# The order of high and low matmuls in the experts' third to eighth group: pairs once a unit, once a half or twice a half, the other k-tiles in turn

## The chip, the cores and the metric

The kernel runs on one core of a Trainium2 chip. The metric is the device time of one execution in microseconds, the median of several runs. The names of the engines are those of the profile: PE (TensorE matmul), PEld (its weight load), DVE (VectorE), ACT (ScalarE), POOL (GpSimd), SP (SyncE, which issues the weight DMAs).

## What is computed

A sequence of 256 tokens with 2048 features passes two blocks in fp32. The first block is a norm, a projection, a pooling mixer beside a gated recurrence, a projection back, and then a layer of 16384 single-neuron experts. The second block has attention, a depthwise convolution, gates and a feed-forward of 8192 features. The part that the change touches is the layer of experts:

```python
u = jnp.take(peer_u, expert, axis=0)
act = jax.nn.gelu(jnp.einsum('chkd,cd->chk', u, zc))
v = jnp.take(peer_v, expert, axis=0)
w = (gate * act.astype(jnp.float32)).astype(zc.dtype)
return jnp.einsum('chk,chkd->cd', w, v).astype(zc.dtype)
```

The kernel computes it densely: all 16384 experts in eight groups of 2048, with a gate that is zero where a token has not chosen the expert.

## The kernel before

All large products are cut into 544 **units**, numbered in the order in which they run. A unit makes 128 output features for 256 tokens. It has two **halves** (p = 0, 1) of 8 **k-tiles** of 128 x 128 weights, so 16 k-tiles. `STAGE` tells for each unit the stage, its number i in the stage, and the group c. In the layer of experts each group c (0 to 7) has 16 units "u" (first product, operand `ZA`) and 16 units "v" (second product, operand `ZB`). The third to eighth group (c = 2 to 7) are the units 120 to 311, and u and v stages follow one another, 16 units each. Later stages in that form are the feed-forward's "up" and "dn" (units 416 to 543).

To keep fp32 precision with fp32r operands, a weight tile is split: `hi` is the rounded weight, `lo` is the rest. The operand is split in the same way and stands as 512 columns, 256 rounded and 256 of rest. A k-tile is therefore two matmuls into one PSUM bank `G`: `high` (L413, `hi` by all 512 columns) and `rest` (L417, `lo` by the first 256 columns). They take 128 x 128 weights each, so each has a weight load of its own.

**Weights.** SP loads one half (512 KB) into a ring of 8 `raw` buffers, and waits for `s_mm`, by which PE tells that a half is done. ACT rounds it into a ring of 7 `hi` buffers (L676). DVE subtracts into `lo`, which lies over `raw` (L1054). `walk` fixes where ACT and DVE prepare halves (two a unit, about two and a half units ahead of PE) between the parts of the evacuation.

**Results.** There are four banks. ACT copies the columns 256 to 511 out (L683) and DVE adds them to the first 256 (L1060). For a unit u of group 2 on, POOL scales, ACT takes gelu, POOL multiplies by the gate, ACT rounds to `ZB` and DVE makes the rest (L1125). A v unit then adds to `X`. The first v unit of a group waits for its operand k-tile by k-tile (`operand_ready`, semaphore `s_zu`).

**The order on PE.** `half` (L437) issues the 8 k-tiles of a half in steps. In a step of 1 it issues high, low. In a step of 2 it issues high, high, low, low, which is called a **pair** here; several k-tiles one by one are **in turn**. PE waits for the high weights ahead of the first high matmul (`s_hi`), and for the low weights ahead of the first low one (`weights_ready`, `s_lo`). `at_once` (L426) gives the step. Before the change it is 2 in the u units of groups c >= 2 and in all v units but the first of a group (i = 0), where it is 1. In the "up" and "dn" stages it is 1. Three places with several units at once go through `group` and take all in turn.

Of the kernel before, what the change touches and what calls it, by code (L numbers as in the profile page):

```python
# [36 lines left out]
F0, SG, MG, YO = 312, 352, 384, 400  # L37
# [127 lines left out]
def build(nc, ins, out):  # L165
    ctx = ExitStack()
    with ctx:
# [80 lines left out]
        qkv, VT, mask, neg = zb["qkv"], zb["VT"], zb["mask"], zb["neg"]  # L248
# [60 lines left out]
        def weights(u, p):  # L309

            st, i, c = STAGE[u]
            ks = range(8 * p, 8 * p + 8)
            if st == "lx":
                return ins["w_in"][8 + i, p], ZA, ks
            if st == "pl":
                return ins["w_in"][2 * POOL_G[i // 2] + i % 2, p], ZA, ks
            if st == "gt":
                return ins["w_in"][16 + i, p], ZA, ks
            if st == "ot":
                return ins["w_out"][i, p], ZB, ks if p else OUT_ORDER  # L320
            if st == "wq":
                return ins["wq"][i, p], ZA, ks
            if st == "u":
                return ins["pu"][16 * c + i, p], ZA, ks
            if st == "v":
                return ins["pv"][i, 2 * c + p], ZB, ks
            if st == "gb":
                return ins["w_in2"][32 + i, p], ZA, ks
            if st == "ga":
                return ins["w_in2"][24 + i, p], ZA, ks  # L330
            if st == "qkv":
                return ins["w_in2"][8 * c + i, p], ZA, ks
            if st == "sg":
                return ins["w_in2"][40 + 16 * c + i, p], ZA, ks
            if st == "mg":
                return ins["w_sc"][i, p], ZB, ks
            if st == "yo":
                return ins["w_o"][i, p], ZA, ks
            if st == "up":
                return ins["w_up"][16 * c + i, p], ZA, ks  # L340
            return ins["w_down"][i, 2 * c + p], ZB, ks
# [28 lines left out]
        def tensor_program(pe):  # L370
            def operand_ready(u, k):
                st, i, c = STAGE[u]
                if u == LX:
                    pe.wait_ge(s_zx, k + 1)
                elif u == OT and k < 8:
                    pe.wait_ge(s_zp, OUT_ORDER.index(k) + 1)
                elif u == OT:
                    pe.wait_ge(s_zg, k - 7)
                elif u == WQ:
                    pe.wait_ge(s_zh, k + 1)  # L380
                elif u in VB[:2] and k % 2 == 0:
                    pe.wait_ge(s_za, 8 * c + k // 2 + 1)
                elif u in VB[2:]:
                    pe.wait_ge(s_zu, 16 * (c - 2) + k + 1)
                elif u == F0:
                    pe.wait_ge(s_zi, k + 1)
                elif u == MG and k < 8:
                    pe.wait_ge(s_zo, k + 1)
                elif u == MG:
                    pe.wait_ge(s_zc, k - 7)  # L390
                elif u == YO:
                    pe.wait_ge(s_zm, k + 1)
                elif u == M0:
                    pe.wait_ge(s_zr, MIX_OF[k] + 1)
                elif u in DNB:
                    pe.wait_ge(s_zf, 16 * c + k + 1)

            def weights_ready(h):
                pe.wait_ge(s_lo, h + 1)

            def bank_free(b):
                if b >= 4:
                    pe.wait_ge(s_join, b - 3)

            def high(u, p, k, G, first):

                w = hi[POS[u][p] % NW][:, k % 8, :]
                Z = weights(u, p)[1]
                if u == N - 1:
                    pe.matmul(G[:, 0:256], w, Z[:, k, 0:256], start=first, stop=False, skip_group_check=True)  # L410
                    pe.matmul(G[:, 0:256], w, Z[:, k, 256:512], start=False, stop=False, skip_group_check=True)
                else:
                    pe.matmul(G[:, 0:512], w, Z[:, k, :], start=first, stop=False, skip_group_check=True)  # L413

            def rest(u, p, n, k, G, last):

                m = pe.matmul(G[:, 0:256], lo[POS[u][p] % NRAW][:, k % 8, :], weights(u, p)[1][:, k, 0:256], start=False,  # L417
                              stop=last, skip_group_check=True)
                if n == 7:
                    m.then_inc(s_mm, 1)  # L420
# [2 lines left out]
                high(u, p, k, G, first)  # L423
                rest(u, p, n, k, G, last)

            def at_once(u):  # L426

                st, i, c = STAGE[u]
                if st in ("ot", "v", "mg", "yo"):
                    return 2 if i else 1  # L430
                if st == "u":
                    return 2 if c >= 2 else 1
                if st in ("gb", "ga", "qkv", "sg"):
                    return 2 if u > F0 else 1
                return 1

            def half(u, p):  # L437
                apart = STAGE[u][0] == "mg"
                b = BANK[u] + (p if apart else 0)
                start, stop = apart or p == 0, apart or p == 1  # L440
                if start:
                    bank_free(b)
                ks = list(enumerate(weights(u, p)[2]))
                step = at_once(u)
                for x in range(0, 8, step):
                    for n, k in ks[x:x + step]:
                        operand_ready(u, k)
                        if n == 0:
                            pe.wait_ge(s_hi, POS[u][p] + 1)
                        high(u, p, k, GB[b % 4], n == 0 and start)  # L450
                    if x == 0:
                        weights_ready(POS[u][p])
                    for n, k in ks[x:x + step]:
                        rest(u, p, n, k, GB[b % 4], n == 7 and stop)

            def group(u):
                units = range(u, u + GROUPS[u])
                for w in units:
                    bank_free(BANK[w])
                for p in range(2):  # L460
                    for n, k in enumerate(range(8 * p, 8 * p + 8)):
                        operand_ready(u, k)
                        for w in units:
                            if n == 0:
                                weights_ready(POS[w][p])
                            product(w, p, n, k, GB[BANK[w] % 4], p == 0 and n == 0, p == 1 and n == 7)
# [113 lines left out]
            for u in range(N + 1):  # L580
# [5 lines left out]
                if u in GROUPS:  # L586
                    group(u)
                elif u not in INSIDE:
                    half(u, 0)
                    if 68 <= u < 84:  # L590
                        spread(2 * (u - 68))
                    half(u, 1)
# [1151 lines left out]
        @block.tensor  # L1744
        def _(e):
            tensor_program(e)
# [73 lines left out]
```

## Time and profile before

| | |
|---|---|
| median of 3 runs | 3238.07 us (3237.05 to 3240.23) |
| the profiled execution | 3243.61 us, span 3241.8 us |
| PE busy | 3161.9 us, 98% of the span |
| PEld busy | 2762.4 us, 85% |
| DVE, ACT, POOL busy | 2180.3, 1693.5, 676.1 us |
| granted TensorE clock, mean | 0.99 |
| HBM | 189 GB/s over the span |
| high matmuls (L413) | 52% of the chain that ended last |
| low matmuls (L417) | 26% of that chain |

Matmuls overlap: a high one is shown as 0.40 us long though the next may start 0.23 us after it. So the starts are read here, not the lengths. In the timeline two matmuls of one kind in a row are merged into one line (x2), which makes pairs easy to see: a line with x2 highs, a line with x2 lows.

### The profile page before, as it was taken

How to read it: one execution, taken by the hardware profiler on the slowest of the kernel's cores; microseconds unless marked ns; L12 is line 12 of the kernel's file. 1: busy time of each engine (PE TensorE's matmuls, PEld its weight loads, DVE VectorE, ACT ScalarE, POOL GpSimd, SP SyncE). 2: the span in 40 equal slices, each digit the busy share in tenths (PEclk: the TensorE clock that was granted, in tenths of full speed). 3: DMA queues.
4: the chain of work that ended last, by engine and by line, in shares of the span. 5: the costliest groups of instructions: out<-in, count | busy, mean ns of one | idle time of the engine just before them, and what ended most of it. 6: DMA issues, size and time to landing. Idle time of an engine off the chain costs nothing.

```text
span 3241.8 us, 46963 instructions
## 1 busy us (share of the span) xinstructions
PE 3161.9 (98%) x18222; PEld 2762.4 (85%) x18222; DVE 2180.3 (67%) x3000; ACT 1693.5 (52%) x2629; POOL 676.1 (21%) x690
## 2 busy tenths in 40 slices
PE   8999989999999999999999999999998999999998
PEld 7788878888888888888888888888887888888887
DVE  7857999864655555565646569999675855555564
ACT  6554457544544445454545655566656544444444
POOL 1423320321312222131313410000242100000003
PEclk9999989999999999999999999999999999999999
DMA  6555547656666666566666665555665566666664
GB/s 241 156 189 177 181 150 234 232 184 211 189 215 189 215 189 215 188 215 189 189 215 189 189 187 162 174 163 184 189 191 163 170 190 191 191 188 190 190 191 138
DMA packets 177853, 615.35 MB, mean 190 GB/s; under 512 B 18272, under 2 KB 35040, under 8 KB 176224
## 3 DMA queue, kind: packets, MB, share of 16 engines
q1 hardware_dynamic: 157824, 572.59, 56.1%
q10 hardware_dynamic: 19808, 39.76, 3.5%
q8 instruction: 145, 2.38, 0.3%
q14 instruction: 76, 0.62, 0.1%
HBM read 593.41 MB, written 18.87 MB: 189 GB/s over the span
## 4 chain that ended last, share of the span: by engine, by line
PE 78%; DVE 13%; issue 4%; ACT 2%; POOL 2%; DMA 1%; ACTq 0%; DVEq 0%; POOLq 0%
PE G L413 52%; PE G L417 26%; DVE lo L1054 5%; DVE CV L1362 2%; DVE oneB L1337 1%; ACT hi L676 1%; DVE tS L1114 1%; DVE oneA L1339 1%; DVE tS L1060 0%; ACT oneB L853 0%; POOL tS L1552 0%; POOL X L1572 0%; DVE XC L1101 0%; POOL acc L1577 0%; DMA raw<-in_pv 0%
## 5 line engine op out<-in xcount | busy, mean ns | idle before, releaser
L413 PE MATMUL G<-ZA,hi 128*128 128x512 f32 x5120 | 1704.1, 398 | 23.5 <-DVE lo L1054 10.8
L1054 DVE TENSOR_TENSOR lo<-raw,hi 128x1024 fp32r<-128x1024 f32 x1088 | 1399.6, 1307 | 301.0 <-ACT hi L676 300.4
L417 PE MATMUL G<-ZA,lo 128*128 128x256 f32 x5120 | 1190.4, 279 | 0.0
L413 PE MATMUL G<-ZB,hi 128*128 128x512 f32 x3568 | 1165.4, 396 | 8.2 <-DVE ZB L1350 4.9
L676 ACT ACTIVATE hi<-raw 128x1024 fp32r<-128x1024 f32 x1088 | 1116.1, 1051 | 76.8 <-DMA raw<-in_pv 37.2
L417 PEld LDWEIGHTS G<-ZA,lo 128*128 128x128 f32 x5120 | 967.3, 189 | 129.9
L413 PEld LDWEIGHTS G<-ZA,hi 128*128 128x128 f32 x5120 | 862.5, 189 | 121.7 <-issue 17.8
L417 PE MATMUL G<-ZB,lo 128*128 128x256 f32 x3584 | 803.6, 278 | 0.0
L417 PEld LDWEIGHTS G<-ZB,lo 128*128 128x128 f32 x3584 | 676.0, 189 | 106.3
L683 ACT ACTIVATE tA<-G 128x256 f32<-128x256 f32 x559 | 212.3, 380 | 949.7 <-PE G L417 948.9
L413 PEld LDWEIGHTS G<-ZB,hi 128*128 128x128 f32 x3568 | 587.5, 189 | 61.5 <-DVE ZB L1117 3.6
L1060 DVE TENSOR_TENSOR tS<-G,tA 128x256 f32<-128x256 f32 x336 | 141.4, 421 | 245.8 <-ACT tA L683 244.1
L1552 POOL TENSOR_TENSOR tS<-tS,R 128x256 f32<-128x256 f32 x152 | 149.1, 981 | 584.1 <-DVE tS L1060 584.1
L1060 DVE TENSOR_TENSOR X<-G,tA 128x256 f32<-128x256 f32 x128 | 54.3, 425 | 298.1 <-POOL tA L1590 298.1
L1590 POOL TENSOR_TENSOR tA<-tA,X 128x256 f32<-128x256 f32 x128 | 101.9, 796 | 548.2 <-ACT tA L683 548.2
L1623 POOL TENSOR_TENSOR tA<-tA,Y 128x256 f32<-128x256 f32 x47 | 34.7, 738 | 602.5 <-ACT tA L683 602.5
L1060 DVE TENSOR_TENSOR Y<-G,tA 128x256 f32<-128x256 f32 x79 | 33.6, 425 | 164.6 <-POOL tA L1623 126.5
L1586 POOL TENSOR_TENSOR tS<-tS,Gc 128x256 f32<-128x256 f32 x96 | 123.2, 1283 | 50.8 <-ACT tS L717 50.8
L1362 DVE SCALAR_TENSOR_TENSOR CV<-UC,col,CV 128x256 f32<-128x256 f32 x240 | 116.0, 484 | 6.9
L529 PE MATMUL M<-oneB,oneA 128*128 128x128 f32 x512 | 65.8, 284 | 13.5 <-DVE oneA L1339 13.3
L529 PEld LDWEIGHTS M<-oneB,oneA 128*128 128x128 f32 x512 | 62.2, 198 | 17.3 <-DVE oneA L1339 15.6
L853 ACT ACTIVATE oneB<-oneB,IJG 128x128 f32<-128x128 f32 x128 | 41.0, 391 | 50.1 <-DVE oneB L1337 50.1
(271 smaller groups left out, 1366.4 us busy)
## 6 DMA issues: line engine op xcount, KB each, us to landing
raw<-in_pu SPq DMA_DIRECT2D x256, 512.0 KB, 3.6
raw<-in_pv SPq DMA_DIRECT2D x256, 512.0 KB, 3.8
raw<-in_w_in SPq DMA_DIRECT2D x192, 512.0 KB, 3.6
raw<-in_w_up SPq DMA_DIRECT2D x128, 512.0 KB, 4.2
raw<-in_w_down SPq DMA_DIRECT2D x128, 512.0 KB, 4.3
raw<-in_w_out SPq DMA_DIRECT2D x32, 512.0 KB, 3.6
raw<-in_wq SPq DMA_DIRECT2D x32, 512.0 KB, 3.5
g_scratch<-stage ACTq DMA_DIRECT2D x16, 1024.0 KB, 4.8
```

Source lines behind the costliest of these rows:

```text
L413: pe.matmul(G[:, 0:512], w, Z[:, k, :], start=first, stop=False, skip_group_check=True)
L417: m = pe.matmul(G[:, 0:256], lo[POS[u][p] % NRAW][:, k % 8, :], weights(u, p)[1][:, k, 0:256], start=False, stop=last, skip_group_check=True)
L529: t = pe.matmul(M[:, 128 * n:128 * n + 128], oA[k % 2][:, 4 * v + n, :], oB[k % 2][:, 4 * v + n, :], start=True, stop=True, skip_group_che ...
L676: act.activation(hi[w][:, :, :], raw[r][:, :].rearrange("p (k n) -> p k n", k=8), ACT.Copy).then_inc(s_hi, 1)
L683: act.activation(tA[b % 3][:, :], GB[b % 4][:, 256:512], ACT.Copy).then_inc(s_low, 1)
L853: act.activation(oB[k % 2][:, n, :], oB[k % 2][:, n, :], ACT.Copy, scale=IJG[:, 2, 8 * k + n:8 * k + n + 1]).then_inc(s_oga, 1)
L1054: dve.tensor_tensor(lo[r][:, :, :], raw[r][:, :].rearrange("p (k n) -> p k n", k=8), hi[w][:, :, :].bitcast(F32), ALU.subtract).then_inc(s ...
L1060: dve.tensor_tensor(dst, GB[b % 4][:, 0:256], tA[b % 3][:, :], ALU.add).then_inc(s_join, 1)
L1362: dve.scalar_tensor_tensor(out=CV[:, j, :], in0=b[:, k:k + 256], scalar=w, in1=CV[:, j, :], op0=ALU.mult, op1=ALU.add).then_inc(s_dw, 1)
L1552: pool.tensor_tensor(b, b, R[:, :], ALU.mult).then_inc(s_scl, 1)
L1586: pool.tensor_tensor(b[:, :], b[:, :], Gc[:, :, i], ALU.mult).then_inc(s_gm2, 1)
L1590: pool.tensor_tensor(t[:, :], t[:, :], X[:, i, :], ALU.add).then_inc(s_vx, 1)
```

## The change

`at_once` now gives the list of the steps of a half instead of one step, and `half` walks this list. For the u and v units of the groups c = 2 to 7 (i = 0 of the v stages included) the lists are new:

- c = 2, 3: one pair and then six k-tiles in turn in the first half, eight in turn in the second;
- c = 4, 5: one pair and six in turn in each half;
- c = 6, 7: a pair, two in turn, a pair, two in turn in each half.

All other units keep their order. The matmuls, their operands and the sum's terms are the same.

```diff
-            def at_once(u):
+            def at_once(u, p):
 
                 st, i, c = STAGE[u]
-                if st in ("ot", "v", "mg", "yo"):
-                    return 2 if i else 1
-                if st == "u":
-                    return 2 if c >= 2 else 1
-                if st in ("gb", "ga", "qkv", "sg"):
-                    return 2 if u > F0 else 1
-                return 1
+                if st in ("u", "v") and c >= 2:
+                    if c < 4:
+                        return (2, 1, 1, 1, 1, 1, 1) if p == 0 else (1,) * 8
+                    return (2, 1, 1, 1, 1, 1, 1) if c < 6 else (2, 1, 1, 2, 1, 1)
+                if st in ("ot", "mg", "yo", "v") and i or st in ("gb", "ga", "qkv", "sg") and u > F0:
+                    return (2,) * 4
+                return (1,) * 8
...
                 ks = list(enumerate(weights(u, p)[2]))
-                step = at_once(u)
-                for x in range(0, 8, step):
+                x = 0
+                for step in at_once(u, p):
                     for n, k in ks[x:x + step]:
...
                     for n, k in ks[x:x + step]:
                         rest(u, p, n, k, GB[b % 4], n == 7 and stop)
+                    x += step
```

## Rows read from the trace of the kernel before

**Rows 1.** The page, part 1: busy time and share of the span, instructions.

```profile
PE 3161.9 (98%) x18222; PEld 2762.4 (85%) x18222; DVE 2180.3 (67%) x3000; ACT 1693.5 (52%) x2629; POOL 676.1 (21%) x690
```

**Rows 2.** Windows: length, PE, PEld, DVE, ACT, POOL busy, clock, DMA share, GB/s.

```profile
813.69:902.86 89.17, 89.17 (x514) 77.80 (x513) 56.92 (x63) 49.10 (x78) 31.07 (x31) 1.00 0.61 189
902.86:992.13 89.27, 89.27 (x515) 77.86 (x513) 44.07 (x49) 37.47 (x50) 13.88 (x17) 1.00 0.64 212
2783.39:2872.14 88.75, 88.75 (x514) 77.59 (x513) 43.88 (x50) 37.21 (x49) 11.07 (x15) 1.00 0.61 190
```

**Rows 3.** Groups by line, 813.69 to 1884.33 us, PE: count | busy, mean | idle before.

```profile
L413 PE MATMUL G<-ZB,hi 128*128 128x512 f32 x1536 | 486.2, 396 | 0.0
L413 PE MATMUL G<-ZA,hi 128*128 128x512 f32 x1537 | 482.8, 395 | 0.0
```

**Rows 4.** Timeline of PE (start, length): two pairs; last pair, then v's unit 0.

```profile
813.69 0.63 PE L413 MATMUL G<-ZA,hi 128*128 128x512 f32 x2
814.16 0.39 PE L417 MATMUL G<-ZA,lo 128*128 128x256 f32 x2
814.39 0.62 PE L413 MATMUL G<-ZA,hi 128*128 128x512 f32 x2
814.85 0.40 PE L417 MATMUL G<-ZA,lo 128*128 128x256 f32 x2
...
902.17 0.62 PE L413 MATMUL G<-ZA,hi 128*128 128x512 f32 x2
902.63 0.40 PE L417 MATMUL G<-ZA,lo 128*128 128x256 f32 x2
902.86 0.40 PE L413 MATMUL G<-ZB,hi 128*128 128x512 f32 x1
...
903.21 0.40 PE L413 MATMUL G<-ZB,hi 128*128 128x512 f32 x1
...
903.57 0.40 PE L413 MATMUL G<-ZB,hi 128*128 128x512 f32 x1
```

**Rows 5.** Timeline of PE: end of that unit 0, its last k-tile, two pairs.

```profile
908.16 0.40 PE L413 MATMUL G<-ZB,hi 128*128 128x512 f32 x1
...
908.51 0.64 PE L413 MATMUL G<-ZB,hi 128*128 128x512 f32 x2
908.99 0.40 PE L417 MATMUL G<-ZB,lo 128*128 128x256 f32 x2
909.23 0.62 PE L413 MATMUL G<-ZB,hi 128*128 128x512 f32 x2
```

**Rows 6.** Timeline of PE: last pair of mg, yo's unit 0 in turn, next pair.

```profile
2408.49 0.63 PE L413 MATMUL G<-ZB,hi 128*128 128x512 f32 x2
2408.96 0.39 PE L417 MATMUL G<-ZB,lo 128*128 128x256 f32 x2
2409.18 0.40 PE L413 MATMUL G<-ZA,hi 128*128 128x512 f32 x1
...
2409.53 0.39 PE L413 MATMUL G<-ZA,hi 128*128 128x512 f32 x1
...
2409.88 0.40 PE L413 MATMUL G<-ZA,hi 128*128 128x512 f32 x1
...
2414.73 0.62 PE L413 MATMUL G<-ZA,hi 128*128 128x512 f32 x2
2415.19 0.40 PE L417 MATMUL G<-ZA,lo 128*128 128x256 f32 x2
```

**Rows 7.** Timeline of PE: first high of units 418 and 428, both in turn.

```profile
2526.64 0.40 PE L413 MATMUL G<-ZA,hi 128*128 128x512 f32 x1
...
2583.17 0.40 PE L413 MATMUL G<-ZA,hi 128*128 128x512 f32 x1
```

**Rows 8.** Timeline of DVE: the last k-tile of unit 136's operand.

```profile
907.54 0.41 DVE L1125 TENSOR_TENSOR ZB<-tS,ZB 128x256 fp32r<-128x256 f32 x1
```

## Prediction, made before the change was run

> **What bounds the kernel now.** I read the page's busy shares first: PE is busy 98% of the span, DVE 67%, ACT 52% [rows 1]. Then the windows of the stages that the change touches. The experts' third to eighth groups are 12 stretches of 16 units (third group's u units, its v units, and so on) and lie between 813.69 and 1884.33 us. In the two that are shown PE is busy for the whole stretch, 89.17 of 89.17 us and 89.27 of 89.27 us, at a granted clock of 1.00 (the 2.4 GHz level) [rows 2]. In the list by line of that whole time the idle time ahead of the high matmuls (L413) is 0.0 us [rows 3]. So nothing that PE waits for can be won or lost here. What is left is how fast PE takes its own queue, and the order of the matmuls is all that the change edits.
>
> **What an order costs.** A k-tile is one high matmul (512 columns) and one low one (256). A unit has 16. Paired (high, high, low, low) they take 89.17 us / 256 k-tiles = 348.3 ns each. In the feed-forward's stretch from 2783.39 us, with as many matmuls but taken in turn (high, low), it is 88.75 / 256 = 346.7 ns [rows 2]. Read alone, this says that each k-tile taken out of a pair wins 1.6 ns.
>
> But the same order in turn has a second, slower rate in this trace. From 2526.64 to 2583.17 us lie ten units of the first feed-forward group in turn, without a stop: 56.53 us / 160 = 353.3 ns [rows 7]. And a v stretch is 0.10 us longer than a u stretch [rows 2] because its unit 0 is in turn, and slow: from 902.86 to 908.51 us, 5.65 us / 16 = 353.1 ns [rows 4, 5]. In the slow rate the high matmuls start 0.35 and 0.36 us apart and all show 0.40 us [rows 4]. In the fast one they show 0.40 and 0.39 us by turns, and a unit takes 5.55 us, from 2409.18 to 2414.73 us [rows 6].
>
> **What picks the rate.** Pairs come in two kinds that follow one another without exception in an undisturbed stretch. The merged rows show a long pair (highs 0.63 us, lows 0.39) and a short pair (0.62, 0.40) [rows 4]. Their starts, counted out in ns, give 697.5 and 695.8 ns, and two of them are 4 x 348.3 ns. There are 11 places where an order in turn follows pairs without a stop; call k-tiles in turn, one behind the other, a series. At 9 the last pair is short and the series in turn is slow: ahead of seven v units 0, of the first wq unit and of F0. One is at 902.17 us [rows 4]. At 2 the last pair is long and the series is fast. One is at 2408.49 us [rows 6], the other at 2320.04 us. Both kinds of series cross units and halves without changing. After a fast series comes a short pair (2414.73 us [rows 6]). After a slow series comes an odd pair of 713.3 ns (0.64 us highs, at 908.51 us), and then a short one (909.23 us) [rows 5]. So the odd pair leaves things as a long pair does. PE carries a phase of a few ns, and a pair flips it: **long pair, fast series, short pair, slow series, long or odd pair, fast series.** I choose to forecast by this chain, since it gives the length of all 12 stretches as they are: 6 x 89.17 + 6 x 89.27 = 1070.64 us.
>
> **The change part by part.** A slow series of n k-tiles costs 350.8, 360.8, 349.2 ns and then 350.0, 360.8, 349.2 in turn. All series have an even length.
> - Third and fourth group, 64 units, one pair and 14 in turn. A fast unit is 699.2 + 14 x 346.7 = 5552.5 ns. A slow unit is 695.8 + 4951.7 = 5647.5. They alternate, mean 5600.0 against 16 x 348.3 = 5573.3 now: +26.7 ns x 64 = +1.7 us.
> - Fifth and sixth, a pair and 6 in turn a half. A fast half is 696.7 + 2080.0 = 2776.7 ns, a slow one 695.8 + 2120.8 = 2816.6. A unit is 5593.3: +20.0 x 64 = +1.3 us.
> - Seventh and eighth, a pair and 2 in turn, four times a unit. Fast 699.2 + 693.3 = 1392.5 ns, slow 695.8 + 711.7 = 1407.5. A unit is 5600.0: +26.7 x 64 = +1.7 us.
> - The six v units 0 were slow throughout (5650.7 ns, and 17 ns more in the odd pair behind each). Now they are like the others: -0.6 us.
>
> The sum is +4.1 us. The pair after a slow series of 2, 6 or 14 is in no row: before, all such series had 16. Its bounds are 695.8 ns (the short pair) and 713.3 (the odd pair). I take 699.2, and 696.7 after six. The slow series repeats every three k-tiles, and the odd pair starts where the 360.8 ns k-tile would have begun. These pairs start elsewhere in the three, so they should not carry its 10 ns. All 223 of them at the upper bound give +3.3 us more (+7.4 in all). At the lower bound it is 0.5 us less.
>
> **Edits at nothing.** The low matmul of a half's first k-tile needs the low weights. It keeps its pair ahead of it, except in the second halves of the third and fourth group, where it comes 0.23 us earlier. In no row of these stretches does PE wait for weights [rows 3]; if that cover were gone, a half would pay at most those 0.23 us. A v unit 0 waits for its operand k-tile by k-tile. The last (DVE L1125) ends at 907.95 us and its matmul starts at 908.16 [rows 8, 5]. A fast unit 0 would come there up to 0.10 us sooner, and 0.21 us cover it. SP, ACT, DVE and POOL keep their order, and only their waits for PE move, by ns. Code ahead of 813.69 us is unchanged. Later, stops can leave a series in the other phase by chance: the ten slow units above are worth 160 x 6.7 ns = 1.1 us either way.
>
> [...] The rows say that the order moves a k-tile between 346.7 and 353.3 ns. [...]
>
> **The rivals.**
> - *In turn is always fast here* (the phase costs nothing). For it: 2783.39 us on, and the two fast places. Against it: 9 places of 11. A unit would be 5550, 5553 and 5560 ns in the three parts: 64 x (23 + 20 + 13) ns = 3.6 us, and 0.6 from the units 0, so -4.2: 3233.9 us.
> - *A pair after a slow series doesn't flip the phase* (slower). The place is each pair behind a slow series of 2, 6 or 14. For it: the only pair seen there came after 16. Against it: that one did flip. If so, all series are slow, a unit is 80, 63 and 80 ns longer: 14.3 - 0.6 = +13.7 us, 3251.8 us. All slow is 9.6 us over my half slow; the sum passes +6.5 us, and so turns slower, once five in eight of the series are slow where I count four. If it holds only for series of 2 and 14, it is +10.8 (3248.9 us).
> - *The order makes no difference*, or its parts cancel: 0, 3238.1 us. [...]
>
> **How the numbers follow.** The profiled execution has a span of 3241.8 us and took 3243.6, 0.17% over the median of 3238.07 us; a difference of ns a unit carries over as it is. Forecast: 3238.07 + 4.1 = **3242.2 us**, chance 0.65. Always fast 0.12, no flip (whole or in part) 0.13, no difference 0.06, something else 0.04. About 0.2% is what a measurement of this kernel can tell from no change: 6.5 us, so under 3231.6 or over 3244.5. Always fast ends inside. From the forecast 0.06 lies over the upper bound, by the odd pair's price. So faster 0.03, same 0.78, slower 0.19. The range goes from 3233.0 (always fast, and a chance phase) to 3247.0 (the odd pair everywhere, and a chance phase). It leaves out the no-flip rival.
>
> **What would show it.** The stretches: 89.60 us in groups three, four, seven and eight, 89.49 in five and six, against 88.8 to 89.0 (always fast) and 90.2 to 90.5 (no flip). The timeline: short pair, then highs of 0.40 us only, 0.35, 0.36, 0.35 us apart; long pair, then 0.40 and 0.39 by turns. PE idle at 0.0 still. I am wrong if a series after a short pair is fast, if a pair after 2 or 14 leaves the next series slow, or if PE stops in these stretches.

## The result

The changed kernel takes 3247.98 us (median of 9 runs, 3246.49 to 3257.45) where the kernel before, run beside it, takes 3239.99 us (9 runs). The ratio is 1.0029, with a 95% interval of 1.0018 to 1.0039: slower, by some 9.4 us (5.8 to 12.6), or 8.0 us by the two medians. The prediction was 3242.2 us with a range up to 3247.0, 4.1 us over its base of 3238.07 us. It was wrong: the time lies 1 us above the range, the change was to make no difference that can be measured, and the mechanism that decided was the rival given 0.13.

The granted clock is 1.00 in all stretches of both kernels below. First the windows of the kernel after: groups three (u, v), five (u, v), seven (u), and the feed-forward stretch. Columns as in [rows 2].

```profile
808.96:899.30 90.34, 90.34 (x514) 78.53 (x513) 56.89 (x63) 49.14 (x78) 31.10 (x31) 1.00 0.59 187
899.30:989.65 90.35, 90.35 (x515) 78.54 (x513) 44.51 (x49) 37.56 (x50) 14.27 (x17) 1.00 0.64 210
1170.34:1259.84 89.50, 89.50 (x515) 78.05 (x514) 56.70 (x63) 49.10 (x78) 31.14 (x31) 1.00 0.59 188
1259.84:1349.37 89.53, 89.53 (x515) 78.01 (x513) 44.09 (x49) 37.48 (x50) 13.83 (x17) 1.00 0.64 212
1528.36:1618.38 90.02, 90.02 (x515) 78.66 (x514) 56.62 (x63) 49.11 (x78) 31.07 (x31) 1.00 0.60 187
2786.30:2875.04 88.74, 88.74 (x514) 77.60 (x513) 44.04 (x50) 37.20 (x49) 11.06 (x15) 1.00 0.61 191
```

PE is busy for the whole of each stretch, as before [rows 2], and the stretches are longer. The feed-forward's is not (88.74 against 88.75). The list by line over the twelve stretches shows no idle time ahead of the high matmuls, as [rows 3]:

```profile
L413 PE MATMUL G<-ZA,hi 128*128 128x512 f32 x1536 | 524.5, 397 | 0.0
L413 PE MATMUL G<-ZB,hi 128*128 128x512 f32 x1536 | 524.5, 397 | 0.0
```

Against the forecast and its rivals, in us a stretch:

| stretches | before | forecast | always fast | no flip (all) | after |
|---|---|---|---|---|---|
| groups 3, 4 | 89.17 / 89.27 | 89.60 | 88.8 | 90.5 | 90.35 |
| groups 5, 6 | 89.17 / 89.27 | 89.49 | 88.9 | 90.2 | 89.49 to 89.53 |
| groups 7, 8 | 89.17 / 89.27 | 89.60 | 89.0 | 90.5 | 90.01 to 90.03 |
| all twelve | 1070.64 | 1074.8 | 1066.4 | 1084.3 | 1079.49 |

The twelve stretches (808.96 to 1888.45 us) are 8.85 us longer than before, which lies between the 8.0 us of the medians and the 9.4 us of the ratio. The span of the profiled execution grew by 2.9 us only (3241.8 to 3244.7). The unchanged code ahead of unit 120 took 808.96 us in place of 813.69 in this one execution, and what follows the stretches took 1.2 us less. Over all profiled executions of this study unit 120 starts between 807.86 and 813.69 us, so single spans say little here, and stretches are compared.

**Where the slow series came from.** The timeline of PE (start, length) in the kernel after, first the entry, then the second unit of group three:

```profile
808.26 0.63 PE L413 MATMUL G<-ZB,hi 128*128 128x512 f32 x2
808.73 0.39 PE L417 MATMUL G<-ZB,lo 128*128 128x256 f32 x2
808.96 0.63 PE L413 MATMUL G<-ZA,hi 128*128 128x512 f32 x2
809.42 0.40 PE L417 MATMUL G<-ZA,lo 128*128 128x256 f32 x2
809.65 0.40 PE L413 MATMUL G<-ZA,hi 128*128 128x512 f32 x1
...
810.00 0.40 PE L413 MATMUL G<-ZA,hi 128*128 128x512 f32 x1
...
814.60 0.63 PE L413 MATMUL G<-ZA,hi 128*128 128x512 f32 x2
815.07 0.40 PE L417 MATMUL G<-ZA,lo 128*128 128x256 f32 x2
815.30 0.40 PE L413 MATMUL G<-ZA,hi 128*128 128x512 f32 x1
...
815.65 0.40 PE L413 MATMUL G<-ZA,hi 128*128 128x512 f32 x1
...
816.01 0.40 PE L413 MATMUL G<-ZA,hi 128*128 128x512 f32 x1
```

Before, the last pair ahead of unit 120 was a short one. Here it is long (0.63 and 0.39), so the first pair of unit 120 is short (0.40 lows) and a slow series follows. That entry is chance. The code ahead of unit 120 is the same in nine of the ten kernels traced here, and the last pair there is a long one in three of the traces and a short one in six. A stop of PE in an earlier stage may set it; which one was not followed.

The second unit shows what the forecast got wrong. Behind a slow series of 14 stands a pair at 814.60 us. From each of its four starts to the next one it is 236, 227, 113 and 119 ns, together 695 ns. And the next series is slow again, its highs 0.35 and 0.36 us apart, all 0.40 us long. The pair did not flip the phase.

In the fifth group a pair does flip it, behind a slow series of 6 (at 1173.16 us; such pairs take 696 to 697 ns), and the fast series behind it shows its 0.40 and 0.39 by turns:

```profile
1170.34 0.62 PE L413 MATMUL G<-ZA,hi 128*128 128x512 f32 x2
1170.81 0.40 PE L417 MATMUL G<-ZA,lo 128*128 128x256 f32 x2
1171.04 0.40 PE L413 MATMUL G<-ZA,hi 128*128 128x512 f32 x1
...
1173.16 0.63 PE L413 MATMUL G<-ZA,hi 128*128 128x512 f32 x2
1173.63 0.39 PE L417 MATMUL G<-ZA,lo 128*128 128x256 f32 x2
1173.86 0.40 PE L413 MATMUL G<-ZA,hi 128*128 128x512 f32 x1
...
1174.20 0.39 PE L413 MATMUL G<-ZA,hi 128*128 128x512 f32 x1
...
1174.55 0.40 PE L413 MATMUL G<-ZA,hi 128*128 128x512 f32 x1
```

### The profile page after: what moved, and what is told of

Read it like the earlier page. It is cut to its first block, busy times and chain, and to the rows that moved or that the text cites. A ratio compares the mean times of both kernels' runs of the same rounds, so it can differ in the third digit from the quotient of the medians.

```text
span 3244.7 us, 46963 instructions
## 1 busy us (share of the span) xinstructions
PE 3167.5 (98%) x18222; PEld 2767.7 (85%) x18222; DVE 2183.3 (67%) x3000; ACT 1696.3 (52%) x2629; POOL 674.5 (21%) x690
## 4 chain that ended last, share of the span: by engine, by line
PE 78%; DVE 15%; issue 3%; ACT 2%; POOL 1%; DMA 1%; ACTq 0%; DVEq 0%; POOLq 0%
PE G L413 51%; PE G L417 26%; DVE lo L1055 6%; DVE CV L1363 3%; DVE oneB L1338 1%; DVE tS L1115 1%; ACT hi L677 1%; DVE tS L1061 1%; DVE oneA L1340 1%; ACT oneB L854 0%; POOL X L1573 0%; POOL acc L1578 0%; DVE XC L1102 0%; DVE oneB L1343 0%; ACT tA L684 0%
## 5 line engine op out<-in xcount | busy, mean ns | idle before, releaser
L413 PE MATMUL G<-ZA,hi 128*128 128x512 f32 x5120 | 1748.9, 399 | 23.4 <-DVE lo L1055 10.7
L417 PE MATMUL G<-ZA,lo 128*128 128x256 f32 x5120 | 1285.8, 280 | 0.0
L413 PE MATMUL G<-ZB,hi 128*128 128x512 f32 x3568 | 1199.3, 396 | 3.6 <-DVE ZB L1351 3.5
L413 PEld LDWEIGHTS G<-ZA,hi 128*128 128x128 f32 x5120 | 903.0, 189 | 171.2 <-issue 17.3
L417 PE MATMUL G<-ZB,lo 128*128 128x256 f32 x3584 | 886.2, 279 | 0.0
L413 PEld LDWEIGHTS G<-ZB,hi 128*128 128x128 f32 x3568 | 621.1, 188 | 102.2 <-DVE ZB L1351 3.6
```

## The experiments

After the result the theory (P) was: PE carries a phase; an order in turn keeps the rate that the pair before it left; and a pair behind a slow series of n k-tiles flips the phase or not according to n. A **stop** is a short wait of PE for an operand; it can throw the phase too. The rivals of (P) were: the place decides (L, the other engines' work in these groups makes an order in turn slow), and each change from in turn to a pair costs (S). The edits are shown against the changed kernel. "Twelve" is the length of the twelve stretches in the profiled execution, against 1070.64 us before.

### One pair between two equal kernels

First kernel. Unit 120 brings PE into one phase whichever way it is entered; the rest is in turn:

```diff
+                if u == UB[2]:
+                    return (2, 2, 1, 1, 1, 1) if p == 0 else (1, 1, 1, 1, 2, 2)
                 if st in ("u", "v") and c >= 2:
-                    if c < 4:
-                        return (2, 1, 1, 1, 1, 1, 1) if p == 0 else (1,) * 8
-                    return (2, 1, 1, 1, 1, 1, 1) if c < 6 else (2, 1, 1, 2, 1, 1)
+                    return (1,) * 8
```

> Unit 120 is taken as two pairs, eight k-tiles in turn, two pairs; all other units of the groups three to eight are in turn. Theory P (PE carries a phase; a series in turn keeps the rate that the pair before it left, and this unit 120 ends in the same phase whichever way it is entered): every k-tile from unit 121 on takes 346.7 ns, each stretch of 16 units 88.75 us, the twelve 1065.1 us against 1070.6 before, the time 5.5 us under before (about 3234.5 us). Theory L (place: in these groups the other engines' work makes an order in turn slow, 353.3 ns, whatever stands before it): stretches of 90.45 us, +14.7 us. Theory S (each change from in turn to pair costs, and there is none left here): also 88.75 us.

Second kernel, the same and a pair at the head of unit 121:

```diff
+                if u == UB[2] + 1 and p == 0:
+                    return (2, 1, 1, 1, 1, 1, 1)
```

> As the first of this call, but the first two k-tiles of unit 121 are a pair; all else from there on is in turn as there. Theory P: the one pair flips the phase, so every k-tile behind it takes 353.3 ns, each stretch 90.45 us, the twelve 1085.3 us, the time 14.6 us over before (about 3254.6 us) and 20 us over its neighbour, for one pair. Theory L: the same as its neighbour, 90.45 us. Theory S: the same as its neighbour but for one change of order, 88.75 us a stretch.

Windows of the first (stretches 1, 3, 4 and 5), then of the second (1, 3 and 12):

```profile
812.65:901.41 88.76, 88.76 (x515) 77.61 (x513) 57.04 (x63) 49.20 (x78) 31.14 (x31) 1.00 0.62 190
990.21:1078.96 88.75, 88.75 (x515) 78.25 (x514) 56.70 (x63) 49.22 (x78) 31.10 (x31) 1.00 0.61 192
1078.96:1169.36 90.40, 90.40 (x515) 78.46 (x513) 44.40 (x49) 38.97 (x50) 14.80 (x17) 1.00 0.65 210
1169.36:1259.81 90.45, 90.45 (x515) 78.48 (x513) 56.64 (x63) 49.26 (x78) 31.03 (x31) 1.00 0.61 186
```

```profile
809.08:899.48 90.40, 90.40 (x514) 78.38 (x513) 56.88 (x63) 49.09 (x78) 31.00 (x31) 1.00 0.60 186
989.94:1080.39 90.45, 90.45 (x515) 78.48 (x513) 56.61 (x63) 49.09 (x78) 31.03 (x31) 1.00 0.60 187
1804.02:1894.47 90.45, 90.45 (x515) 78.48 (x513) 51.10 (x64) 61.90 (x110) 39.66 (x45) 1.00 0.60 187
```

In the first three stretches the two kernels run the same 48 units but for one pair, and are 88.8 against 90.4 us. By chance the two traces enter unit 120 in different phases (its eight in turn are fast in the first, slow in the second), and both leave it with a long pair, so the unit does set the phase. The place (L) is thereby out for these, and so is the count of changes (S). In the second kernel all twelve are slow: 1085.39 us where 1085.3 was expected, and the time is 3252.35 us (4 runs), 1.0040 (1.0025 to 1.0055) of before.

But the first kernel did not stay fast: from the fourth stretch on it is slow, its twelve are 1080.34 us, and its time is 3254.98 us (5 runs), ratio 1.0052 (1.0038 to 1.0066). The expected 5.5 us under before did not come. Only the profiled execution, 3250.7 us, shows where it turned. The median is 2.6 us above that of the second kernel, though the twelve stretches in the trace are 5.05 us shorter; what the other four executions did is not shown. The timeline of PE at the end of the v unit 0 of group four, and the DVE row of its last operand, show why:

```profile
1083.81 0.39 PE L413 MATMUL G<-ZB,hi 128*128 128x512 f32 x1
...
1084.16 0.45 PE L413 MATMUL G<-ZB,hi 128*128 128x512 f32 x1
1084.44 0.28 PE L417 MATMUL G<-ZB,lo 128*128 128x256 f32 x1
1084.56 0.39 PE L413 MATMUL G<-ZB,hi 128*128 128x512 f32 x1
...
1084.91 0.40 PE L413 MATMUL G<-ZB,hi 128*128 128x512 f32 x1
...
1085.27 0.40 PE L413 MATMUL G<-ZB,hi 128*128 128x512 f32 x1
```

```profile
1083.63 0.41 DVE L1126 TENSOR_TENSOR ZB<-tS,ZB 128x256 fp32r<-128x256 f32 x1
```

The last high matmul starts at 1084.16 us, 0.12 us behind the end of its operand (1084.04; 0.11 counted out in ns) where it was 0.21 before [rows 8, 5]. It shows 0.45 us in place of 0.39 or 0.40, and its low part follows after 0.28 us in place of 0.23. The only wait that the program has ahead of this matmul is the one for its operand, and in this trace the same delay stands in the v units 0 of groups three and four, which came early, and not in the other four. This stop of 0.05 us costs little by itself. Behind it PE is in the other phase, and the next 8 x 16 units and more, with no pair among them, stay there. In group three the same stop left the series fast (stretch 3, 88.75); why one stop throws the phase and the other doesn't was not found.

### A pair and six everywhere; two pairs and eight

```diff
                 if st in ("u", "v") and c >= 2:
-                    if c < 4:
-                        return (2, 1, 1, 1, 1, 1, 1) if p == 0 else (1,) * 8
-                    return (2, 1, 1, 1, 1, 1, 1) if c < 6 else (2, 1, 1, 2, 1, 1)
+                    return (2, 1, 1, 1, 1, 1, 1)
```

> All units of the groups three to eight as the fifth and sixth in the changed kernel: a pair and six in turn in each half, so 384 pairs and 384 changes of order. Theory P, with the rule that a pair behind a slow series flips the phase after 6 (a multiple of three) and doesn't after 2 or 14 (two more than one): stretches of 89.49 us, the twelve 1073.9 us, +3.3 us against before and 5.5 us under the changed kernel. Theory S (changes of order cost; there are more of them than in the third and fourth group of the changed kernel, 32 a stretch against 16 at 90.35 us): at least 90.4 us a stretch. Theory L (the place decides: the groups three, four, seven and eight are slower in themselves): 89.5 in five and six alone, 90.0 to 90.4 in the others.

```diff
                 if st in ("u", "v") and c >= 2:
-                    if c < 4:
-                        return (2, 1, 1, 1, 1, 1, 1) if p == 0 else (1,) * 8
-                    return (2, 1, 1, 1, 1, 1, 1) if c < 6 else (2, 1, 1, 2, 1, 1)
+                    return (2, 2, 1, 1, 1, 1) if p == 0 else (1, 1, 1, 1, 2, 2)
```

> All units of the groups three to eight as two pairs, eight in turn, two pairs. Theory P: from a long pair's phase the four pairs lead back to it and the eight are fast (346.7 ns); from the other, the pair behind a slow series of eight (two more than a multiple of three) takes 695 ns and does not flip, the next one flips, and the unit ends right: so all units are fast from the second on, 5560 ns each, stretches of 88.96 us, the twelve 1067.6 us, 3.0 us under before. Without the rule for eight (a pair always flips): the unit keeps the phase it is entered in, and the stretches are 88.96 or 89.8 us by chance. Theory S: four pairs a unit as in groups seven and eight of the changed kernel, but one change of order in place of four, about 89.4 us.

Windows of "a pair and six" (stretches 1, 9 and 10), then of "two pairs and eight" (2 and 3):

```profile
810.29:899.78 89.49, 89.49 (x514) 77.96 (x513) 56.99 (x63) 49.23 (x78) 31.05 (x31) 1.00 0.61 189
1526.29:1615.78 89.49, 89.49 (x514) 77.96 (x513) 56.69 (x63) 49.11 (x78) 31.05 (x31) 1.00 0.61 188
1615.78:1705.29 89.51, 89.51 (x515) 77.97 (x513) 44.19 (x49) 38.88 (x50) 13.86 (x17) 1.00 0.65 212
```

```profile
900.11:989.28 89.17, 89.17 (x515) 77.72 (x513) 44.17 (x49) 37.59 (x50) 13.84 (x17) 1.00 0.65 212
989.28:1078.24 88.96, 88.96 (x515) 77.71 (x513) 56.61 (x63) 49.15 (x78) 31.03 (x31) 1.00 0.61 189
```

Six in every place gives 89.49 or 89.51 us, in the groups that had 90.35 and 90.02 in the changed kernel too. So neither those places nor the number of changes of order (32 a stretch here, 16 in group three of the changed kernel) made them slow; the length of the series did. The twelve are 1074.00 us (1073.9 expected), the time 3242.8 us (10 runs), ratio 1.0015 (1.0005 to 1.0025), so +4.9 us. The expected +3.3 us lies inside the interval.

Two pairs and eight leads back to the fast side each time: u stretches 88.96 (first 89.02), as expected. The v stretches are 89.17, not 88.96. A v unit 0 that ends in pairs needs its last operand sooner still. Its last pair takes 853 ns in place of 697, a stop of 0.16 us, and the eight in turn of the next unit are slow, which makes the other 0.05 us. Then the unit's own pairs have led back. The twelve are 1068.86, and the time is 3238.08 us (10 runs), ratio 0.9999 (0.9989 to 1.0009). The expected 3.0 us under before lies inside that interval, near its lower end, and the time can't be told from no change.

### Holding the fast side

The same unit of two pairs, eight, two pairs, now behind each stop only; all else in turn:

```diff
+                if u == UB[2] or u - 1 in VB[2:]:
+                    return (2, 2, 1, 1, 1, 1) if p == 0 else (1, 1, 1, 1, 2, 2)
                 if st in ("u", "v") and c >= 2:
-                    if c < 4:
-                        return (2, 1, 1, 1, 1, 1, 1) if p == 0 else (1,) * 8
-                    return (2, 1, 1, 1, 1, 1, 1) if c < 6 else (2, 1, 1, 2, 1, 1)
+                    return (1,) * 8
```

> The first kernel of the call before went fast for three stretches and then slow for nine: its v unit 0, faster by 0.1 us, reached its last operand too early, PE stopped for 0.05 us, and the fourth stretch was slow. Here unit 120 and the second v unit of each of the six groups (the one behind that stop) are two pairs, eight in turn, two pairs, and all else in the six groups is in turn. Theory P (phase, flipped by pairs, thrown by stops, and set by this unit): u stretches 88.75 us, v stretches 88.8 to 89.0 (a stop of 0.05 to 0.10 us, the four pairs +0.01, the unit behind the stop up to 0.09 slower), the twelve about 1065.9 us, so 4.7 us under before and 13.6 us under the changed kernel. Theory L (in turn is slow in the later groups by their place): as in that first kernel, 90.45 us from the fourth stretch on.

Windows (stretches 2, 3 and 12), then the stop in the v unit 0 of group three:

```profile
898.55:987.43 88.88, 88.88 (x514) 77.65 (x513) 44.06 (x49) 37.90 (x50) 14.05 (x17) 1.00 0.64 214
987.43:1076.18 88.75, 88.75 (x515) 77.60 (x513) 56.70 (x63) 49.09 (x78) 31.12 (x31) 1.00 0.59 190
1786.70:1875.58 88.88, 88.88 (x514) 77.60 (x513) 50.99 (x64) 61.88 (x110) 39.72 (x45) 1.00 0.59 189
```

```profile
903.75 0.44 PE L413 MATMUL G<-ZB,hi 128*128 128x512 f32 x1
904.03 0.28 PE L417 MATMUL G<-ZB,lo 128*128 128x256 f32 x1
```

All twelve stretches are fast, to the last: 1065.79 us (1065.9 expected), 4.85 under before, with the stop (0.44 us long, its low part 0.28 us behind) still there in each v unit 0. The time is 3234.93 us (11 runs) against 3238.63 before beside it, ratio 0.9989 (0.9980 to 0.9998). Six such units, of the 192, are all that this kernel has over the first one of these experiments, and its stretches are 14.6 us shorter. The ratios of this kernel and of the all-slow one (1.0040) are some 16.5 us apart where their stretches are 19.6 apart, so the whole times of many executions bear the two rates out.

The same, further out:

```diff
-                if u == UB[2] or u - 1 in VB[2:]:
+                if u == UB[2] or u - 1 in VB[1:] or u in (VB[0] + 2, MG + 1, M0 + 2, M0 + 13):
                     return (2, 2, 1, 1, 1, 1) if p == 0 else (1, 1, 1, 1, 2, 2)
-                if st in ("u", "v") and c >= 2:
+                if st in ("u", "v") and c >= 2 or st in ("v", "mg", "yo"):
                     return (1,) * 8
```

> As its neighbour, and the same done in the v units of the first two groups, in mg, in yo, and by two such units in the first feed-forward group. Theory P: besides the 4.7 us, 0.35 us in each v stage and 0.4 us each in mg and yo (15 units of 26 ns), and up to 1.1 us in the feed-forward group where that was slow: 6 to 7 us under before, about 3232 us. Against it: stops in those stages can throw the phase behind the setting unit, each with up to 1.6 us.

3231.82 us (11 runs, 3230.03 to 3234.72), ratio 0.9975 (0.9963 to 0.9987), so 6.8 us or 8 us under before by the medians or the ratio. The twelve are 1065.65 us, and units 384 to 431 (mg, yo, the first feed-forward group's up) take 283.72 us against 285.86 before; in the other eight traces, where they run unchanged, they take 284.34 to 286.19. The whole interval lies below 1, so this version is faster than the kernel before, by about 0.25%, and than the changed kernel.

### Pair, four, pair

```diff
+                if u == UB[2]:
+                    return (2, 2, 1, 1, 1, 1) if p == 0 else (1, 1, 1, 1, 2, 2)
                 if st in ("u", "v") and c >= 2:
-                    if c < 4:
-                        return (2, 1, 1, 1, 1, 1, 1) if p == 0 else (1,) * 8
-                    return (2, 1, 1, 1, 1, 1, 1) if c < 6 else (2, 1, 1, 2, 1, 1)
+                    return (2, 1, 1, 1, 1, 2)
```

> All halves of the groups three to eight are pair, four in turn, pair; unit 120 (two pairs, eight, two pairs) sets the entry. Theory P with the rule by length (behind a slow series of 4, one more than a multiple of three, the pair is the odd one of 713 ns and flips, as it did behind 16): entered from a long pair's phase, each half is short pair, slow four, odd pair, so the phase repeats and every half is slow: 2820 ns, stretches of 90.24 us. Were the pair behind four like the one behind six (697 ns), 89.98; were it like the one behind 2, 8 and 14 (695 ns, no flip), the halves would be fast from the second unit on or vary, 88.96 to 89.9. Theory S (cost by the number of changes of order, 2 a half as in groups seven and eight of the changed kernel): about 90.0.

One run, 3245.96 us. Windows of the first four stretches, then the timeline of PE at the head of unit 121 (short pair, slow four, odd pair with highs of 0.64 us):

```profile
808.53:898.75 90.22, 90.22 (x514) 78.34 (x513) 56.97 (x63) 49.08 (x78) 31.12 (x31) 1.00 0.57 187
898.75:987.86 89.11, 89.11 (x514) 77.74 (x513) 44.06 (x49) 37.43 (x50) 14.24 (x17) 1.00 0.63 213
987.86:1076.82 88.96, 88.96 (x514) 77.70 (x513) 56.71 (x63) 49.07 (x78) 31.14 (x31) 1.00 0.58 190
1076.82:1167.14 90.32, 90.32 (x514) 78.28 (x513) 44.16 (x49) 37.58 (x50) 13.90 (x17) 1.00 0.62 210
```

```profile
814.15 0.63 PE L413 MATMUL G<-ZA,hi 128*128 128x512 f32 x2
814.62 0.40 PE L417 MATMUL G<-ZA,lo 128*128 128x256 f32 x2
814.85 0.40 PE L413 MATMUL G<-ZA,hi 128*128 128x512 f32 x1
...
816.26 0.64 PE L413 MATMUL G<-ZA,hi 128*128 128x512 f32 x2
816.74 0.40 PE L417 MATMUL G<-ZA,lo 128*128 128x256 f32 x2
```

The first stretch is the expected slow cycle (90.22). The rule for four holds: the pair behind it is the odd one, 713 ns. Then the stop at the end of the v unit 0 throws the phase, and the same instruction order takes 89.11 and 88.96 us, the value of the fast side, until the stop of the next v unit 0 throws it back (90.32). The stops were not in the expectation. The same happens in groups five and six; groups seven and eight stay slow, behind a stop in each v unit 0. So one order has two lengths here, 1.3 us apart a stretch, and it changed between them only at a stop, of under 0.2 us.

### Other steps

```diff
                 if st in ("u", "v") and c >= 2:
-                    if c < 4:
-                        return (2, 1, 1, 1, 1, 1, 1) if p == 0 else (1,) * 8
-                    return (2, 1, 1, 1, 1, 1, 1) if c < 6 else (2, 1, 1, 2, 1, 1)
+                    return (4, 4) if c < 4 else (8,) if c < 6 else (3, 3, 2)
```

> Other orders, one look: groups three and four take four high and four low parts at a time, groups five and six eight and eight, groups seven and eight three, three and two. Theory P says nothing of their rates but that each order settles into a cycle; if the lows alone are what is slow or quick in a place, the stretches lie outside the 88.75 to 90.45 us of in turn, and if the mix of neighbours (high to high, low to low) sets them, all lie within 0.5 us of the 89.17 us of pairs. The first v unit with eight and eight needs its last operand about 0.8 us sooner and stops for it.

One run, 3245.83 us: u stretches of 89.81 us (four and four), 89.39 (eight) and 89.49 (three, three, two); v stretches of 90.14 to 90.17, 90.24 to 90.25 and 89.62. All of the u stretches are slower than pairs (89.17) and than a fast order in turn (88.75), and lie within 0.7 us. They stay inside the 88.75 to 90.45 us of in turn, so this run doesn't bear out that the lows alone decide. The v stretch of eight and eight is 0.85 us over its u stretch, the expected stop. That all orders stay within 0.5 us of pairs fails for four and four (0.64), so the mix of neighbours is no sufficient account either. What rate each settles into wasn't followed further.

## Why the prediction was wrong, by its own steps

- **PE is the bound and nothing else moves: right.** PE is busy for 100% of the stretches before and after.
- **Two rates in turn (346.7 and 353.3 ns), 348.3 paired; the last pair picks the rate: right.** In the second kernel of the experiments twelve stretches at 353.3 ns came out within 0.1 us of the sum, and so did those at the fast rate in the kernel of "Holding the fast side" (1065.79 against 1065.9). What the step left open is that a stop picks the rate too.
- **A pair behind a slow series always flips the phase: wrong, and this is the step that failed.** It rested on the one length in the trace, 16. That a pair after 2 or 14 leaves the next series slow was one of my own signs of being wrong, and it came. Measured in all the traces, leaving out pairs next to a stop:

| slow series before the pair | pairs seen | the pair, ns | flips |
|---|---|---|---|
| 2, 14 (two over a multiple of three) | 318 | 695 | no |
| 8 (two over) | 20 | 695 | no |
| 6 (a multiple of three) | 254 | 696 to 697 | yes |
| 4 (one over) | 249 | 713 | yes |
| 16 (one over) | 6 | 713 | yes |

  I had reasoned that these pairs start elsewhere in the cycle of three than the odd one and so would not carry its 10 ns, and stopped there. The same thought should have said that they may leave another phase too. I gave 0.65 to a behaviour seen at one of the cycle's three places. Why a pair at one place of the cycle flips the phase and at another doesn't is not shown.
- **Group by group.** Fifth and sixth: +20.0 ns a unit forecast, 89.49 us measured, exact. Third and fourth: forecast +26.7 ns a unit, measured +73.6 (90.35 / 16 = 5646.9 ns: a pair of 695 and a slow 14 of 4951.7). Seventh and eighth: forecast +26.7, measured +53.5 (5626.8: four times 695 + 711.7).
- **The price of the unseen pair** was 699.2 with bounds 695.8 and 713.3. It is 695, 0.8 ns under the lower bound. (The lower bound would have taken 0.6 us off the sum, not 0.5.) The no-flip rival for series of 2 and 14 alone stood at +10.8 us because its 80 ns a unit put that pair at 702; with 695 for its 318 pairs it is 2.1 us less, +8.7, against 8.85 measured.
- **A v unit 0 has 0.21 us of cover: wrong in general, harmless here.** In the changed kernel most of them are slow and don't stop. In the first experiment 0.10 us less of it was enough for a stop of 0.05 us. Cover that is read as the time from the producer's end to the matmul's start is not all free. In the stopped units the distance from the operand's end to the matmul's start and the delay of its low part add up to the same 0.16 us (0.11 + 0.05 in the first kernel, 0.12 + 0.04 in "Holding the fast side"), so about 0.05 us of the 0.21 was free. The price of the stop was not its length but the phase behind it, 1.7 us a stretch.
- **The entry.** I took the phase at unit 120 as fixed. It was the other one in the profiled execution after. By the table above its orders reach the slow side from either entry, within a unit or two, so it should cost the changed kernel next to nothing (the other entry was not seen there). It had no place in the sum.
- **Rivals.** "Always fast" is out: no pattern of the change stays fast. "The order makes no difference" is out too: the first two experiments differ by one pair, and a k-tile by 6.7 ns. The Trainium skill's page TensorE: Matmul & The Clock Gate (section Back-to-back issue gap) gives columns / 2.4 + 2.5 ns as the gap of an isolated warm matmul, and says that in a stream of weight loads and matmuls both set the spacing. By that formula the two matmuls of a k-tile would take 325 ns (an estimate from the page: 213.3 + 106.7 + 5). The runs show 346.7 and 353.3 ns for the same two matmuls, and the formula has no term for what stood before them.
- **Range.** It left out the no-flip rival, whose form for 2 and 14 alone was the right one, and its upper end was 3247.0.

## What to carry to other kernels

Where PE is the bound and matmuls come in a fixed pattern, count the starts in the trace over a few hundred matmuls: one order can have more than one rate. Here a rate lasted until a pair or a stop of PE came. Don't compare two orders by one stretch of each; note what stood before. If a fast rate exists, it may be held by a short piece that leads to it from any phase (here two pairs, eight in turn, two pairs), put behind each place where PE can stop. And a transition seen at one place of a cycle is one observation, not a rule for the others.

## What the runs showed of the hardware

- A high matmul of 512 columns and a low one of 256, with a weight load each, take 346.7 or 353.3 ns in turn at a granted clock of 1.00, and 348.3 ns paired; which of the first two is a matter of history. The slow series repeats every 3 k-tiles (1060 ns), the fast one every 2 (693.3 ns), pairs every 4 (1393.3 ns).
- One pair, once, put all 191 units behind it at the slow rate, 107 ns a unit (16 x 6.7) over the fast one: 1085.39 us for the twelve stretches, where the kernel that holds the fast side has 1065.79, PE shown busy throughout in both.
- A stop of PE of 0.05 us can do the same: nine stretches in the first experiment went slow behind one, though the same stop one group earlier changed nothing.
- An operand that DVE ended 0.20 us or more ahead of the start of its matmul in a v unit 0 cost no stop; one that ended 0.11 to 0.12 us ahead cost 0.04 to 0.05 us.
- What in PE or its operand reads carries the phase was not found. No run here tells.
